# First mixer of a two-layer block on one core: decayed keys before a weight remainder, level 2 before the gate's last piece, and other places for filler matmuls

## What is computed

```python
def hgrn2_chunkwise(q, k, v, log_f):
    """S_t = diag(f_t) S_{t-1} + k_t v_t^T ; o_t = S_t^T q_t, evaluated chunk by chunk."""
    ...
    def step(state, inp):
        q_, k_, v_, b_ = inp
        o_inter = jnp.einsum('bhtk,bhkv->bhtv', q_ * jnp.exp(b_), state)
        ...
        scores = jnp.einsum('bhtsk,bhsk->bhts', q_[:, :, :, None, :] * decay, k_)
        o = o_inter + jnp.einsum('bhts,bhsv->bhtv', scores, v_)
        b_last = b_[:, :, -1, :]
        k_dec = k_ * jnp.exp(b_last[:, :, None, :] - b_)
        state = jnp.exp(b_last)[..., None] * state + jnp.einsum('bhsk,bhsv->bhkv', k_dec, v_)
...
    q, f, i, g = jnp.split(h @ w_in, 4, axis=-1)
...
    o = o * lax.rsqrt(jnp.mean(jnp.square(o), -1, keepdims=True) + RMS_EPS)
    o = o * g_norm_w.astype(jnp.float32) * jax.nn.silu(heads(g))
    return o.reshape(B, S, D).astype(h.dtype) @ w_out
```

## Time and profile before

| | |
|---|---|
| three runs, median (lowest to highest) | 1485.26 us (1483.27 to 1485.62) |
| the profiled execution's own time | 1481.93 us |
| its span in the profile | 1480.1 us |
| TensorE busy | 1445.2 us (98%) |
| VectorE busy | 867.6 us (59%) |
| ScalarE busy | 604.2 us (41%) |
| GpSimd busy | 485.3 us (33%) |
| mean granted TensorE clock | 0.999 |

### The profile page before, as it was taken

The page is one execution under the profiler, slowest core; times in us unless marked ns, Lnnn a source line. Parts: engine busy times, 40 slices in busy tenths (PEclk is TensorE's granted clock), DMA queues, the critical chain, the costliest instruction groups (busy, mean ns, idle before and its releaser), DMA issues.

```text
span 1480.1 us, 23546 instructions
## 1 busy us (share of the span) xinstructions
PE 1445.2 (98%) x9326; PEld 1200.5 (81%) x9326; DVE 867.6 (59%) x1229; ACT 604.2 (41%) x780; POOL 485.3 (33%) x360
## 2 busy tenths in 40 slices
PE   8999998999999999999989999999999999999999
PEld 6887887898888888899767988888888897777677
DVE  7787686576665660155796766656620274565741
ACT  5565654353223222245453442232221355655541
POOL 0000000225544545432231145455454524422222
PEclk9999999999999999999999999999999999999999
DMA  7422122403223233222212122322223312312211
GB/s 222 136 74 87 58 87 96 162 29 114 85 90 109 85 112 115 102 97 70 78 41 74 58 87 85 105 94 92 106 85 113 128 58 85 133 71 72 72 56 59
DMA packets 25631, 136.29 MB, mean 92 GB/s; under 512 B 2600, under 2 KB 7368, under 8 KB 10832
## 3 DMA queue, kind: packets, MB, share of 16 engines
q1 hardware_dynamic: 18288, 124.79, 23.9%
q10 hardware_dynamic: 7264, 10.39, 2.6%
HBM read 130.96 MB, written 4.21 MB: 91 GB/s over the span
## 4 chain that ended last, share of the span: by engine, by line
issue 41%; PE 27%; POOL 24%; DVE 3%; DMA 2%; ACT 1%; DVEq 1%; SPq 0%; POOLq 0%; ACTq 0%
POOL WL L471 15%; POOL WL L480 9%; PE pair L506 7%; PE pair L508 7%; PE pair L507 6%; DMA RAW<-stream 2%; PE pair L1095 1%; PE pair L1082 1%; DVE WL L1672 1%; PE pair L691 1%; PE pair L1014 1%; ACT WH L1201 1%; PE pair L1072 1%; PE pair L720 1%; PE pair L726 0%
## 5 line engine op out<-in xcount | busy, mean ns | idle before, releaser
L506 PE MATMUL pair<-AH,WH 128*128 128x512 f32 (+1 forms) x1240 | 473.3, 382 | 9.9 <-DVE AL L1661 6.9
L471 POOL TENSOR_TENSOR WL<-RAW,WH 128x512 fp32r<-128x512 f32 x228 | 311.7, 1399 | 472.6 <-ACT WH L1201 472.6
L508 PE MATMUL pair<-AH,WL 128*128 128x512 f32 (+1 forms) x1240 | 462.7, 373 | 0.0
L507 PE MATMUL pair<-AL,WH 128*128 128x512 f32 (+1 forms) x1240 | 462.4, 373 | 0.0
L1201 ACT ACTIVATE WH<-RAW 128x2048 fp32r<-128x2048 f32 x106 | 203.0, 1915 | 459.6 <-PE pair L508 450.6
L480 POOL TENSOR_TENSOR WL<-RAW,WH 128x512 fp32r<-128x512 f32 x128 | 173.4, 1386 | 504.1 <-ACT WH L1201 504.1
L506 PEld LDWEIGHTS pair<-AH,WH 128*128 128x128 f32 x1240 | 233.5, 188 | 58.7 <-issue 16.0
L508 PEld LDWEIGHTS pair<-AH,WL 128*128 128x128 f32 x1240 | 233.4, 188 | 42.2
L507 PEld LDWEIGHTS pair<-AL,WH 128*128 128x128 f32 x1240 | 233.7, 188 | 40.8 <-issue 1.9
L2042 DVE TENSOR_SCALAR CA<-pair,PAR 128x512 f32<-128x512 f32 x88 | 67.3, 806 | 147.7 <-PE pair L508 144.7
L506 PE MATMUL pair<-GH,WH 128*128 (+2 forms) x416 | 148.7, 357 | 0.1
(11 more groups left out here) (252 smaller groups left out, 1875.4 us busy)
## 6 DMA issues: line engine op xcount, KB each, us to landing
RAW<-stream SPq DMA_DIRECT2D x114, 1024.0 KB, 4.9
H<-x_t SPq DMA_DIRECT2D x5, 512.0 KB, 7.2
bias_rows<-ROWS ACTq DMA_DIRECT2D x1, 2048.0 KB, 24.3
FBC<-forget_rows ACTq DMA_DIRECT2D x4, 512.0 KB, 3.8
out<-H ACTq DMA_DIRECT2D x8, 256.0 KB, 2.0
H<-x_t SPq DMA_DIRECT2D x1, 1024.0 KB, 10.5
BIAS<-bias_rows ACTq DMA_DIRECT2D x1, 1024.0 KB, 5.9
RAW<-stream SPq DMA_DIRECT2D x3, 256.0 KB, 6.5
```

The source lines that it names most:

```text
L471: pool.tensor_tensor(WL[w][:, part], RAW[raw][:, part], WH[w][:, part].bitcast(F32), ALU.subtract).then_inc(w_lo, 1)
L506: pe.matmul(out_, wh, xh, start=start, stop=False, skip_group_check=shared)
L507: pe.matmul(out_, wh, xl, start=False, stop=False, skip_group_check=shared)
L508: return pe.matmul(out_, wl, xh, start=False, stop=stop, skip_group_check=shared)
```

## The change

Six places, all in the first mixer:

- VectorE, iteration 0: `key_decay(0)` goes ahead of the remainder of chunk 4.
- TensorE, last iteration: `level(2)` goes ahead of `gate(3)`; `mixed(0, 1)` goes from behind level 7 to behind `mixed(0, 0)`, ahead of level 6; `mixed(1, 2)` goes ahead of `outputs`, and `mixed(1, 3)` ahead of `sums`.
- ScalarE, last iteration: `expo` of level 5 ahead of `gate`, `expo` of level 6 ahead of the high part of chunk 17.
- VectorE, last iteration: `scale_qk` of level 5 ahead of `shift` of level 6.

```diff
@@ TensorE, hgrn
                 turn_kd()
-                gate(3)
+                if not last:
+                    gate(3)
                 pe.wait_ge(level_picked, 8 * it + 2)
                 level(2)
-                if not last:
+                if last:
+                    gate(3)
+                else:
                     forget(0)
...
                 if last:
                     mixed(0, 0)
+                    mixed(0, 1)
...
                 if last:
-                    mixed(0, 1)
+                    mixed(1, 2)
                     outputs()
-                    mixed(1, 2)
+                    mixed(1, 3)
                     sums()
-                    mixed(1, 3)
                     mixed(1, 0)
                     mixed(1, 1)
@@ ScalarE, hgrn
                 expo(it, 4)
-                gate(it)
-                expo(it, 5)
-                split_hg(HG_G[it])
-                expo(it, 6)
-                if not last:
+                if last:
+                    expo(it, 5)
+                    gate(it)
+                    expo(it, 6)
+                    split_hg(HG_G[it])
+                else:
+                    gate(it)
+                    expo(it, 5)
+                    split_hg(HG_G[it])
+                    expo(it, 6)
@@ VectorE, hgrn
                 if it == 0:
                     query_decay(0)
+                    key_decay(0)
                 split_lo(HG_F[it + 1] if not last else N_HO)
-                if it == 0:
-                    key_decay(0)
...
-                shift(it, 6)
-                scale_qk(it, 5)
+                if last:
+                    scale_qk(it, 5)
+                    shift(it, 6)
+                else:
+                    shift(it, 6)
+                    scale_qk(it, 5)
                 pick(it, 4)
```

## The result

Median **1487.18 us** (1485.07 to 1490.81, 22 runs) against 1485.07 (1482.34 to 1487.46, 22 runs) of the kernel before beside it: ratio 1.002, 95% interval 1.0013 to 1.0027. The change costs 2.1 us by the medians and 0.20%, 3.0 us, by the ratio. The forecast was no change, 1485.2; the time lies inside its range, but the measurement tells it from no change. The profiled execution took 1486.66 us, span 1484.9, which is 4.8 above before's span: before's profiled run, 1481.93, lies 3 us under its own median, and so the two traces are further apart than the medians.

The account below looks back on a forecast made before the run. TensorE, busy 98% of the span, was taken as the bound, so only its waits could be regained: -0.98 us in iteration 0 and +0.9 in the last make -0.1, 1485.26 to 1485.2 us; range 1482.6 to 1487.6.

Parts of the forecast that it names:

- Decayed keys first: Iteration 0: the product fills VectorE's wait for chunk 4, so TensorE gains 0.98 us, kept until the last iteration.
- rival 2: Iteration 0's gain is lost on the way to a load or wait: +0.9 us, 1486.2 us; chance 0.12.
- Level 2 ahead of gate(3): Last iteration: VectorE's picks come 1.6 us earlier, but the gain ends waiting for chunk_states; cost 0.15 us.
- Scale 5 ahead of shift 6: Last iteration, VectorE: level 5's wait shrinks to about 1.2 us, but scale 6 comes 1.05 later, chunk 17's remainder 1.15.
- rival 1: Last iteration gains, late exponential and chunk 17 not deciding: mix_rest 0.3 us earlier, sum -1.3, 1484.0 us; chance 0.15.
- The fillers: Last iteration, TensorE: moved mixed matmuls fill waits; outputs starts at 253.15, mix_rest at 263.25, 0.85 to 0.9 us later.
- Rival 3: TensorE's clock falls in the wait ahead of outputs: 1487.7 us for twelve matmuls, 1490.1 for twice as many; chance 0.04.
- no single one is longer than the 2.31 that passed: Last iteration: TensorE's new waits, about 1.2, 0.3 and 2.3 us, were taken to leave the clock alone.
- The sum: Whole kernel: -0.98 us from iteration 0 and +0.9 from the last iteration make -0.1 us.

Follow-up runs that it names:

- e1: The kernel before with only iteration 0's decayed keys moved ahead of the remainder of chunk 4: 1483.52 us, ratio 0.9995 to before.
- e8: The kernel before with decayed keys first, load of H[:, 2:4] later, level 2 first, ScalarE's new order, chunk_states ahead of mixed(0, 2): 1481.92 us, ratio 0.9987 to before.
- e3: The change, with SyncE's 512 KB load of H[:, 2:4] moved behind the other two loads of H: 1484.87 us, ratio 1.0006 to before.
- e5: The change with the fillers as before, mixed(0, 1) behind level 7 and mixed(1, 2) behind outputs: 1485.59 us, ratio 1.0010 to before.
- e2: The change without the move of iteration 0's decayed keys: 1488.63 us, ratio 1.0027 to before.
- e6: The change without VectorE's swap, shift 6 again ahead of scale 5: 1485.36 us, ratio 1.0011 to before.
- s4: The change without VectorE's swap and with the load of H[:, 2:4] behind the other loads of H: 1483.64 us, ratio 0.9984 to before.
- d1: The kernel before with three extra subtractions on VectorE ahead of scale 6 in the last iteration: 1485.93 us, one profiled execution.
- quiet: An edit used in several runs: SyncE's 512 KB load of H[:, 2:4] goes behind the other two loads of H, out of the stretch.
- e4: The kernel before with the load of H[:, 2:4] behind the other loads of H: 1482.79 us, ratio 0.9993 to before.
- e7: The kernel before with iteration 0's decayed keys first and the load of H[:, 2:4] behind the other loads of H: 1482.57 us, ratio 0.9977 to before.
- c1: The kernel before with decayed keys first, the load of H[:, 2:4] later and the bias rows' store behind value(0): 1482.21 us, ratio 0.9988 to before.
- d2: The kernel before with three extra subtractions ahead of the last iteration's scale 6, and the load of H[:, 2:4] later: 1488.80 us, one profiled execution.

## Why the prediction was wrong

**Decayed keys first.** The mechanism was right: L699 without a wait. The 0.98 was too high: e1 has 0.7 in the median, and in the change's profile nothing is left at 233 (+0.06), since level 2 waits 1.20 for a pick that stands behind the late remainder, and starts at 58.51, as in before. That is rival 2, which I gave 0.12. "What is queued next on VectorE (shift 3, scale 2, pick 1) moves by more than TensorE does" held only for a load landing when before's profile had it (49.44 + 7.80 = 57.24 for level 2, against 58.51 less 0.98).

**Level 2 ahead of gate(3).** Right: `states` waits 2.12 (forecast "about 2") and starts at 241.15 (240.95, and 0.06 of shift). The gain ends in this wait; e8 shows that it can be used.

**Scale 5 ahead of shift 6.** Right for the data. With the 0.06 taken off: level 5's wait 1.11 (about 1.2), level 5 at 244.23 (244.1), scale 6 at 246.60 (246.4), chunk 17's remainder at 248.40 (248.2), each 0.1 to 0.2 later than summed. The last exponential starts at 245.57, as shift 6 ends, so rival 1 is out.

**The fillers: here the prediction failed.** The step reads "`outputs` starts, at 251.98 + 1.15 = 253.15" and "`mix_rest` ... 263.25". It counts for TensorE only waits for data and banks. The term that is missing is the packet of instructions: it follows scale 6, which I had moved by 1.05 us (1.29 and 1.30 for its halves in the profiles), and comes at 251.14 instead of 247.78, because behind the load it is another 2 us late (3.87 behind scale 6, against 1.86 in e3). TensorE goes on 2.27 us after the packet's start. I had also moved mixed(0, 1) ahead of level 6, so the boundary, a fixed matmul of the sequence, fell on the last two matmuls of level 7, on which pick 7 and `SS` hang; in before it fell on a filler. Measured: `outputs` 256.28, 3.1 us behind the forecast's 253.15 (e5, with the boundary on a filler, 253.71), and `mix_rest` 266.66, 3.4 behind the 263.25.

**Rival 3.** The clock did fall, and it was given 0.04. It fell behind a stall of 4.01 us, not behind the 2.3 us wait that I priced. From 254.15 on, each matmul costs 0.43; five steps of 0.20 us extra ahead of `outputs`, and the windows show full clock again at 257. The bound "no single one is longer than the 2.31 that passed" held for data waits alone. The Trainium skill's warning ("TensorE: Matmul & The Clock Gate", section "Why this matters for your kernels") that gaps between bursts bring the lower level back was right here.

**The sum.** In the profiles, +4.26 us at `mix_rest` against a forecast of -0.1. The 4.4 between them: about 3.1 for the stall and the clock ahead of `outputs`, 0.3 for the matmuls of `outputs` that still ran low, and 1.0 for the gain of iteration 0 that wasn't there. In the medians it is +2.1, by the ratio +3.0, and this fits e2 (the last iteration alone, 0.27%, +4.0) less the 0.7 of e1. Three things have to meet for it, and taking any one away gives back 0.09 to 0.14% of the 0.20, with intervals that overlap the change's, so that it is the traces that show each: the swap (e6), the fillers' places (e5) and the load (e3). With the swap and the load both gone (s4) the ratio is clearly under 1.

Still open: why a packet behind the load sometimes stands 2 us (e1, the change) and sometimes only takes longer (before, e6, d1); and why quiet is worth 0.27% between e6 and s4 when their last iterations differ by 0.5 us in the traces. The two may be one question: the profiled executions of before and of e6 are the fastest of their kernels, so the packet may well be later in most of the others. No trace shows that.

## What to carry to other kernels

Read the waits put down to "issue" as closely as those for data. Some are a wait that the profile can't name (the 0.89 us ahead of `mix_rest`). But one that stays at the same number of the sequence in several versions, with a packet of instructions some 2.3 us ahead of its end, is the engine's wait for its own instructions, and a semaphore wait shortly ahead of such a place delays the packet with it. Before an order is changed, look at what then stands at that place (a filler can take the wait, the last matmul of a chain can't) and at which transfer starts in the same instant. Moving a load that had time out of that stretch gave 0.07 to 0.27% in four pairs (before and e4, the change and e3, e1 and e7, e6 and s4), of which only the last is clear of both intervals; the re-ordering of a whole iteration lost 0.27% (e2).

## What was not expected of the hardware

- The packet of instructions starts 1.80 to 2.11 us behind the start of the product that releases TensorE's wait, and 1.73 in c1, wherever the load doesn't make it late; d1 and d2, with that product delayed, have 1.85 and 2.04. TensorE goes on 2.2 to 2.5 us behind the packet's start, and 2.9 in before and e6 and 3.2 in d1, where the packet itself took 1.60 to 1.73 us instead of 0.93 to 1.22: from the packet's end it is 1.25 to 1.5 us in all fourteen traces with the wait. With the load of 512 KB starting beside it the packet came 2.0 us later in six traces of nine.
- The same wait of 2.3 us ahead of level 5 leaves the clock alone in before, e6, s4 and c1, but in e1, e4, e7, d1 and d2 the clock falls to half for 3.4 us, between 0.2 us ahead of the wait's end (d2) and 1.2 us behind it (e1). In TensorE's timeline of e7 the matmuls are 0.43 apart from 246.40 on, with no other wait between:

```profile
245.04 0.75 PE L690 MATMUL pair<-QT,KT_ 128*32 128x32 f32 x64 [2.31 <-DVE KT_ L1732]
...
246.40 0.63 PE L507 MATMUL pair<-OH,WL 128*128 128x512 f32 x1
246.83 0.63 PE L505 MATMUL pair<-OH,WH 128*128 128x512 f32 x1
247.25 0.63 PE L506 MATMUL pair<-OL,WH 128*128 128x512 f32 x1
```

  One profile in which a wait passed is no proof that it will the next time: I had taken it for one.
